# Spreading the operations of a sparse attention stage, and adding squares before they are summed over partitions

## The reference

```python
# first block, layer 0: gated linear attention, 4 heads of 256 values
o = o * lax.rsqrt(jnp.mean(o * o, axis=-1, keepdims=True) + EPS) * g_out
# first block, layer 1: sparse attention, 16 heads of 64, 4 key heads
kv = (hn @ w_kv).reshape(Bsz, S, 6, NSA_KV_HEADS, NSA_HEAD_DIM).transpose(2, 0, 3, 1, 4)
k_cmp = compress_blocks(kv[0], pe_k, wk1, wk2)
v_cmp = compress_blocks(kv[1], pe_v, wv1, wv2)
o = gates[0] * o_cmp + gates[1] * o_sel + gates[2] * o_win
# second block, both layers: 4 heads of difference attention, 8 of stick-breaking
w = probs(qb1, k1) - lam * probs(qb2, k2)
o_diff = (rms_norm(o_diff, subln) * (1.0 - lam_init)).reshape(b, s, DIFF_WIDTH)
a = jnp.where(mask, jnp.exp(log_beta + after), 0.0)
```

## Time and profile before

| | |
|---|---|
| three runs | 2820.82, 2820.78, 2819.22 us; median 2820.78 |
| profiled execution | 2820.03 us, its span 2818.3 us |
| instructions | 39309 |
| PE busy | 2794.5 us, 99% |
| POOL busy | 2043.4 us, 73% |
| VectorE busy | 1328.5 us, 47% |
| ScalarE busy | 816.2 us, 29% |
| mean granted clock of TensorE | 0.998 |

### The profile page before, as it was taken

The page is one execution under the profiler, slowest core; times in us unless marked ns, Lnnn a source line. Parts: engine busy times, 40 slices in busy tenths (PEclk is TensorE's granted clock), DMA queues, the critical chain, the costliest instruction groups (busy, mean ns, idle before and its releaser), DMA issues.

```text
span 2818.3 us, 39309 instructions
## 1 busy us (share of the span) xinstructions
PE 2794.5 (99%) x14380; PEld 2257.1 (80%) x14380; DVE 1328.5 (47%) x1878; ACT 816.2 (29%) x1470; POOL 2043.4 (73%) x2353
## 2 busy tenths in 40 slices
PE   9999999999999999999999999999999999999999
PEld 7888888888766888888877788888887777888887
DVE  4945666044575576604765553231074545533201
ACT  3342222024475222202435422110043444211101
POOL 7958998768655788877855587777785456877774
PEclk9999999999999999999999999999999999999999
DMA  4213223233200333332212223332332222332232
GB/s 153 77 53 105 96 96 94 96 96 120 68 2 2 98 97 97 97 97 94 86 60 68 68 91 96 97 97 97 97 97 68 66 62 82 95 96 95 96 96 96
DMA packets 66507, 242.59 MB, mean 86 GB/s; under 512 B 7504, under 2 KB 7632, under 8 KB 66384
## 3 DMA queue, kind: packets, MB, share of 16 engines
q1 hardware_dynamic: 66384, 240.95, 26.6%
HBM read 238.82 MB, written 2.10 MB: 85 GB/s over the span
## 4 chain that ended last, share of the span: by engine, by line
PE 96%; DVE 2%; ACT 1%; issue 1%; POOL 0%; DMA 0%; SPq 0%; DVEq 0%; ACTq 0%
PE bank L545 28%; PE bank L547 28%; PE bank L546 28%; PE bank L1018 1%; PE bank L942 1%; PE bank L1199 1%; PE bank L1115 1%; PE bank L1158 1%; PE bank L960 1%; PE bank L1171 1%; PE bank L1096 1%; ACT n_P L1551 1%; PE bank L599 0%; DVE ss L1805 0%; PE bank L1086 0%
## 5 line engine op out<-in xcount | busy, mean ns | idle before, releaser
L504 POOL TENSOR_TENSOR w_lo<-w_raw,w_hi 128x256 fp32r<-128x256 f32 x1780 | 1480.9, 863 | 49.6 <-ACT w_hi L1458 14.6
L545 PE MATMUL bank<-XH,w_hi 128*128 128x512 f32 x2416 | 957.0, 396 | 3.6 <-POOL w_lo L504 2.0
L547 PE MATMUL bank<-XH,w_lo 128*128 128x512 f32 x2416 | 942.5, 390 | 0.0
L546 PE MATMUL bank<-XL,w_hi 128*128 128x512 f32 x2416 | 941.8, 390 | 0.0
L501 POOL CAST w_hi<-w_raw 128x1024 fp32r<-128x1024 f32 x437 | 484.0, 1108 | 622.3 <-DMA w_raw<-weights_dram 621.4
L545 PEld LDWEIGHTS bank<-XH,w_hi 128*128 128x128 f32 x2416 | 454.4, 188 | 104.4 <-issue 9.9
L547 PEld LDWEIGHTS bank<-XH,w_lo 128*128 128x128 f32 x2416 | 454.3, 188 | 96.4
L546 PEld LDWEIGHTS bank<-XL,w_hi 128*128 128x128 f32 x2416 | 454.8, 188 | 93.8 <-issue 2.6
L1820 DVE TENSOR_TENSOR X<-X,bank 128x512 f32<-128x512 f32 x63 | 43.1, 684 | 512.5 <-PE bank L547 512.2
L547 PE MATMUL bank<-hid_h,w_lo 128*128 (+1 forms) x704 | 273.9, 389 | 0.0
L545 PE MATMUL bank<-hid_h,w_hi 128*128 (+1 forms) x704 | 273.9, 389 | 0.0
(11 more groups left out here) (368 smaller groups left out, 3303.3 us busy)
## 6 DMA issues: line engine op xcount, KB each, us to landing
w_raw<-weights_dram SPq DMA_DIRECT2D x445, 512.0 KB, 3.4
x_tok<-x_dram SPq DMA_DIRECT2D x4, 512.0 KB, 5.0
out_dram<-y_tok SPq DMA_DIRECT2D x4, 512.0 KB, 4.1
const_sb<-consts_dram SPq DMA_DIRECT2D x1, 834.0 KB, 12.0
par_sb<-params_dram SPq DMA_DIRECT2D x1, 665.0 KB, 10.5
masks_in<-masks_dram SPq DMA_DIRECT2D x1, 640.0 KB, 13.0
w_raw<-weights_dram SPq DMA_DIRECT2D x2, 256.0 KB, 6.4
y_gain<-gain_out_dram SPq DMA_DIRECT2D x1, 512.0 KB, 4.5
```

Of the source, the lines that this page charges most:

```text
L504: ins = nc.gpsimd.tensor_tensor(w_lo[s][:, rows, :], w_raw[s][:, rows, :], w_hi[s][:, rows, :].bitcast(F32), ALU.subtract)
L545: nc.tensor.matmul(out_ap, w_hi[slot][:, j, :], xh, start=start, stop=False)
L546: nc.tensor.matmul(out_ap, w_hi[slot][:, j, :], xl, start=False, stop=False)
L547: return nc.tensor.matmul(out_ap, w_lo[slot][:, j, :], xh, start=False, stop=stop)
```

## The change

It has five parts. The diff follows, cut to its core.

1. GLA: VectorE adds the two squared tiles of each head, and PE sums four tiles in place of eight.
2. kv stage: the tile units come one place earlier against the compression units; ScalarE's high parts are made later among its other work; PE's last compression unit stands between two turns of values.
3. Query stage and row loop: score rows 2 and 3 are issued in the middle of the last query tile, with their maxima and exponentials ahead of that tile's eviction. The steps of rounds 2 and 3, the turns and the late swaps get other rows.
4. Difference attention: ScalarE keeps the squares in f32 and makes a rounded copy, VectorE the rest, and PE sums both with two matmuls in fp32r against minus one (ScalarE's Ln takes the opposite scale). PE waits also for the rest (`osql`). For head 3 the subtraction is put ahead of the stick-breaking loop on VectorE.
5. `stats(MID)` moves from k = 2 to k = 6 of its tile.

```diff
-KV_UNIT = [START["kv"] + (t if t < 5 else 2 * t - 4) for t in range(U_NSA_KV)]
-CMP_UNIT = [START["kv"] + 5 + 2 * n for n in range(U_CMP)]
+KV_UNIT = [START["kv"] + (t if t < 6 else 2 * t - 5) for t in range(U_NSA_KV)]
+CMP_UNIT = [START["kv"] + (6 + 2 * n if n < 7 else 19) for n in range(U_CMP)]
...
-        CMP_TURN_ROW = (24, 64)
+        CMP_TURN_ROW = (22, 58)
+        SWAP_ROW = (27, 28, 33, 34, 51, 52, 57, 58)
...
                 for k in range(KT):
+                    if between and k == KT // 2:
+                        between(2)
...
-                    if k == 2 and norm == MID:
+                    if k == 6 and norm == MID:
                         stats(norm)
...
                         for h in range(H4):
-                            pe.wait_ge(gs["osq"], 2 * h + 2)
-                            for j in range(2):
-                                mm = nc.tensor.matmul(bank[4 + h][:, :], ones_m, g_osq[:, 2 * h + j, :], start=j == 0, stop=j == 1)
-                            mm.then_inc(gs["on"], 1)
+                            pe.wait_ge(gs["osq"], 8 + h + 1)
+                            nc.tensor.matmul(bank[4 + h][:, :], ones_m, g_osq[:, 2 * h, :], start=True, stop=True)\
+                                .then_inc(gs["on"], 1)
...
-                    if t >= 4:
-                        compress(t - 4)
+                    if t >= 5:
+                        compress(t - 5)
                     if t - 1 in (6, 7, 10):
                         v_turn(t - 1)
+                compress(7)
                 v_turn(11)
...
-                    tile(u0 + t, t % 4, XH2, XL2, ns["xl2"] if t == 0 else None)
+                    tile(u0 + t, t % 4, XH2, XL2, ns["xl2"] if t == 0 else None,
+                         between=scores if t == 8 else None)
...
                     pe.wait_ge(hs["osq"], 4 * ly + h + 1)
+                    pe.wait_ge(hs["osql"], 4 * ly + h + 1)
                     if h:
                         pe.wait_ge(hs["ors"], 4 * ly + h)
-                    nc.tensor.matmul(bank[6][:, :], ones_m, h_osq[:, :], start=True, stop=True).then_inc(hs["on"], 1)
+                    nc.tensor.matmul(bank[6][:, :], negones_r[:, :], h_osq_hi[:, h, :], start=True, stop=False)
+                    nc.tensor.matmul(bank[6][:, :], negones_r[:, :], h_osq_lo[:, :], start=False, stop=True).then_inc(hs["on"], 1)
...
                 for t in range(4):
-                    if t == 2:
+                    if t == 3:
                         compression_high(0)
...
+                k_swap(0)
                 compression_high(1)
-                k_swap(0)
-                compression_high(2)
                 k_swap(1)
                 k_doubled(0)
+                compression_high(2)
+                k_doubled(1)
                 compression_high(3)
...
-                for q in range(2, NSA_ROWS + 8):
-                    if q in (15, 51):
-                        cmp_exp(2 + q // 51)
-                    if 34 <= q < 38:
-                        late_swap(6, q - 34)
-                    if 58 <= q < 62:
-                        late_swap(7, q - 58)
+                for q in range(4, NSA_ROWS + 8):
+                    if q in (13, 49):
+                        cmp_exp(2 + q // 49)
+                    if q in SWAP_ROW:
+                        late_swap(6 + SWAP_ROW.index(q) // 4, SWAP_ROW.index(q) % 4)
...
-                    nc.scalar.activation(h_osq[:, :], bank[3][:, :], ACT.Square).then_inc(hs["osq"], 1)
+                    own(nc.scalar.activation(h_osq[:, :], bank[3][:, :], ACT.Square))
+                    nc.scalar.activation(h_osq_hi[:, h, :], h_osq[:, :], ACT.Copy).then_inc(hs["osq"], 1)
...
+                for h in range(H4):
+                    dve.wait_ge(gs["osq"], 8 + h)
+                    V.tensor_tensor(g_osq[:, 2 * h, :], g_osq[:, 2 * h, :], g_osq[:, 2 * h + 1, :], ALU.add).then_inc(gs["osq"], 1)
                 for f in range(5):
                     gated(f)
...
                 for e in range(8):
+                    if e == 7:
+                        score_weights(0)
+                        score_weights(1)
+                        score_max(2)
+                        score_max(3)
                     dve.wait_ge(s_used, START["nsa_q"] + 1 + e + 1)
...
+                def squares_low(h):
+                    dve.wait_ge(hs["osq"], 4 * ly + h + 1)
+                    V.tensor_tensor(h_osq_lo[:, :], h_osq[:, :], h_osq_hi[:, h, :].bitcast(F32), ALU.subtract).then_inc(hs["osql"], 1)
+
...
                     combine(n)
+                    if n >= 5 and (n - 5) % TT == 0:
+                        squares_low((n - 5) // TT)
...
                 k0 = SB_HEADS * ly
+                squares_low(DIFF_HEADS - 1)
                 for h in range(SB_HEADS):
```

More of the change, by code:

```diff
@@ L355, in build @@
         h_osq = at("h_osq", [P, T], F32, o_sq)
+        h_osq_hi = at("h_osq_hi", [P, 4, T], F32R, o_A + 16384)
+        h_osq_lo = at("h_osq_lo", [P, T], F32R, o_sq)
         h_ors = at("h_ors", [P, T], F32, o_sq + T)
@@ L418, in build @@
             "evac", "rot", "rope", "vT", "vc", "gate", "lp", "lsum", "le", "lam", "s", "mx", "exp", "w", "t", "tc", "pv",
-            "sqs", "skd", "osq", "on", "ors", "od", "odh", "odl", "z", "ln", "soft", "sphi", "sp", "cum", "a", "spv", "osc", "osh", "osl", "mevac", "mt", "m", "mh",
+            "sqs", "skd", "osq", "osql", "on", "ors", "od", "odh", "odl", "z", "ln", "soft", "sphi", "sp", "cum", "a", "spv", "osc", "osh", "osl", "mevac", "mt", "m", "mh",
             "ml")}
@@ L575, in first_tiles, with tile @@
                 mm.then_inc(s_used, 1)
-            def tile(u, b, xh, xl, k_sem=None, k_base=0, norm=None):
+            def tile(u, b, xh, xl, k_sem=None, k_base=0, norm=None, between=None):
                 for k in range(KT):
+                    if between and k == KT // 2:
+                        between(2)
                     if u:
@@ L986, in nsa @@
                         cmp_turn(1, 2)
-                        scores(2)
                 for q in range(4, NSA_ROWS + 6, 2):
@@ L1482, in k_doubled @@
                     ins.then_inc(ns["kd"], 1)
+                k_swap(0)
                 compression_high(1)
-                k_swap(0)
-                compression_high(2)
                 k_swap(1)
                 k_doubled(0)
+                compression_high(2)
+                k_doubled(1)
                 compression_high(3)
-                k_doubled(1)
                 v_copy(0)
@@ L1493, in nsa @@
                 v_copy(1)
+                k_swap(2)
                 compression_high(5)
-                k_swap(2)
-                compression_high(6)
                 k_swap(3)
                 k_doubled(2)
+                compression_high(6)
+                k_doubled(3)
                 compression_high(7)
-                k_doubled(3)
                 v_copy(2)
@@ L1560, in nsa @@
                         cmp_exp((e - 3) // 2)
-                score_exp(0)
-                score_exp(1)
+                for q in range(4):
+                    score_exp(q)
                 cmp_copy(1, 2)
@@ L1749, in d_norm @@
                     act.wait_ge(hs["od"], 4 * ly + h)
-                own(nc.scalar.activation(h_ors[:, :], bank[6][:, :], ACT.Ln, bias=eps_col, scale=1.0 / (2 * DH)))
+                own(nc.scalar.activation(h_ors[:, :], bank[6][:, :], ACT.Ln, bias=eps_col, scale=-1.0 / (2 * DH)))
                 nc.scalar.activation(h_ors[:, :], h_ors[:, :], ACT.Exp, scale=-0.5).then_inc(hs["ors"], 1)
@@ L2266, in nsa @@
                         score_max(1)
-                    if e == 7:
-                        score_weights(0)
-                        score_weights(1)
                 def late_cos(e):
@@ L2280, in late_sum @@
                     V.tensor_tensor(n_q[:, e, :], n_rot[e % 2][:, :], n_t1[:, :], ALU.add).then_inc(ns["rope"], 1)
-                for q in range(2, NSA_ROWS + 9):
+                for q in range(3, NSA_ROWS + 9):
                     if q == 7:
                         cmp_scores(3)
+                    if q in (9, 45):
+                        cmp_max(2 + q // 45)
                     if q in (11, 47):
-                        cmp_max(2 + q // 47)
-                    if q in (13, 49):
-                        cmp_less(2 + q // 49)
+                        cmp_less(2 + q // 47)
+                    if q in (15, 51):
+                        cmp_sums(2 + q // 51)
                     if q in (17, 53):
-                        cmp_sums(2 + q // 53)
-                    if q in (21, 57):
-                        cmp_weights(2 + q // 57)
+                        cmp_weights(2 + q // 53)
                     if q in (39, 63):
@@ L2306, in nsa @@
                         V.tensor_copy(transposed_rows(m), turned_bank(m)).then_inc(ns["tcd"], 1)
-                    if q < NSA_ROWS:
+                    if 4 <= q < NSA_ROWS:
                         score_max(q)
-                    if 3 <= q <= NSA_ROWS:
+                    if q <= NSA_ROWS:
```

## The result

Measured over 20 runs of each kernel, the changed one takes 2824.32 us (2822.17 to 2826.69) and the one before 2819.87 (2815.95 to 2824.03): ratio 1.0016 [1.0010, 1.0022]. So it is a little slower, by about 4.5 us or 0.16%, and that is outside the noise of these runs. I had forecast 3.5 faster, 2817.3, with a range of 2814 to 2821. The profiled execution after took 2822.92 us (span 2821.1), 2.9 more than the profiled one before.

The account below looks back on a forecast made before the run. PE was taken to bound the kernel, through what it issues and waits for. Terms -1.6 - 5.0 - 0.8 - 2.6 - 0.7 - 3.0 + 10.2 = -3.5 gave median 2817.3 us (own range 2814 to 2821; 8 in 10: 2810.5 to 2824.5).

Parts of the forecast that it names:

- Head 3, +10.2: Difference attention, two layers: subtraction ahead of VectorE's stick-breaking loop delays sp, PE pauses and the clock falls; +5.1 each.
- rival (a): Head 3's pause is cheap, short chain and clock holds: 2.9 each instead of 5.1, median 2812.9; chance 0.27.
- the long chain: Head 3: VectorE's chain from L2431 to the end of L2439 at its upper end, 6.4 us; bound 7.1 a layer.
- kv stage, -5.0: Unit order of the kv stage: PE's waits for POOL, n_yh and the V copy go; -5.0, between -5.8 and -1.5.
- Rival (c): Early waits only move, POOL or ScalarE late elsewhere; kv and sparse stages bring 2.6, not 8.4; median 2823.1, chance 0.12.
- GLA, displaced queue "at nothing, up to +1": Gatings and norms behind VectorE's GLA adds come some 2.7 us later, covered by VectorE's gaps: nothing, up to +1.
- The term for the sums: GLA square sums: PE runs 4 matmuls instead of 8 but waits for VectorE's first add; -1.6, from -3.2 to +0.3.
- rival (d): VectorE's adds cost GLA what it gains: 1.6 us more; no chance of its own, within the first case's range.
- Row loop, -2.6: Spread swaps fit ScalarE's gaps, -1.0; the fourth round's turn moves to a row with idle time, about -1.9; -2.6.
- Heads 0 to 2, -3.0: Difference attention, two layers: two rounded matmuls (0.45) replace one f32 matmul (0.95) on PE; -0.5 six times, -3.0.
- Query stage -0.35 against -0.8: Score rows 2 and 3 inside the query tile: the 0.9 wait for n_P goes; -0.8, from -1.6 to +0.3.
- MID -0.7 against -0.7: Norm sum of MID four steps later in its tile: its 0.6 wait for ss goes; -0.7, from 0 to -0.8.

Follow-up runs that it names:

- Experiment 2: Kernel before, with VectorE only waiting for the squares of head 3 ahead of its stick-breaking loop, no instruction added: 2825.78 us, ratio 1.0023.
- Experiment 5: Changed kernel, with ScalarE's high part of the second compression unit (unit 1) made ahead of the first swap: 2824.5 us, ratio 1.0018 to the kernel before.
- Experiment 7: Changed kernel, with only ScalarE's high part of the first compression unit (unit 0) made a turn earlier, as it was: 2823.67 us, ratio 1.0015 to the kernel before.
- Experiment 8: Changed kernel, with compression unit 0's high part a turn earlier and unit 1's ahead of the first swap: 2819.02 us, ratio 0.9999 to the kernel before.
- Experiment 6: Changed kernel, with late swaps at rows 39, 40, 63, 64 instead of 33, 34, 57, 58: 2822.84 us, ratio 1.0011 to the kernel before.
- experiment 3: Changed kernel, with head 3's subtraction moved into head 0's step, behind sp and its tile's eviction: 2820.18 us, ratio 1.0003 to the kernel before.
- experiment 4: Changed kernel, with the four GLA adds ahead of VectorE's eviction of tile 21, on their own semaphore: 2820.94 us, ratio 1.0002 to the kernel before.

## Why the prediction was wrong

**Head 3, +10.2: right.** Measured +4.5 and +5.2. The working held part by part: subtraction ahead of sp, a pause of 3.87 (forecast 4.5), chain 4.3 (4.9), and a slower clock behind it in both layers. Experiment 2 shows the mechanism without any of the new instructions. (Two of its bounds don't come out of its terms: a short chain without the clock gives 2.6, where rival (a) counts 2.9, and the long chain 6.6, where I wrote 7.1.) I had this price and set against it 13.7 us of gains, of which 7.0 came, and 2.0 more were lost in GLA. So the error is in the gains.

**kv stage, -5.0: failed, it brought 2.0.** The failed step is "POOL has that tile ready at about 627 and the next at about 641". The first held (625.81). The next I dated by POOL's own work alone and left out what POOL waits for, ScalarE's high parts. The diff makes them later: it puts `compression_high(0)` one turn later and `compression_high(1)` behind the swap, which waits for VectorE. POOL, with nothing to do from 625.8 on, began the compression unit at 633.24, and PE's tile was ready at 650.26. Experiments 5, 7 and 8 show that these two places, together, are the cause; with both the stage brings 2.0 + 3.9 = 5.9, about my own upper end of 5.8. The waits for n_yh and the V copy did go as forecast. Rival (c), with a chance of 0.12, has this outcome almost to the number: it gave the kv stage, query stage and row loop 2.6 in place of 8.4, and they brought 2.8. It said that POOL or ScalarE would be late, and it was ScalarE. What I had named in its favour, that POOL was busy throughout, was not the reason: POOL stood idle.

**GLA, displaced queue "at nothing, up to +1": failed, +2.0.** The term for the sums is right (-1.6, measured -1.7). What failed is the cover that I counted on behind them, "VectorE had gaps of 1.8 us before the last evictions". The gaps took in most of the adds, but the other instructions grew by 2.0, and the last low part came 2.5 later. The slack at the output product was 2.5 and PE came 1.7 earlier. I had not read that slack at all. This is rival (d), which I had put inside the forecast.

**Row loop, -2.6: failed, -0.45.** The failed step is "two and two with six rows between them fit the gaps", -1.0: they cost 0.78 each at the second pair of both late rotations, and the old places gave back only 0.34 and 1.05, so this part came to +0.2. Experiment 6 takes both costs away by moving these pairs alone. The turn was mis-sized too, -0.8 in place of -1.6 (-1.9, and 0.3 for a late copy). The pause of 1.9 went, but the rows behind it cost 0.7 more than they had behind a pause, with a wait of 0.19 for n_P at 858.36 that was not there, and each of the two turns costs 0.2 more in its new row.

**Heads 0 to 2, -3.0: mis-sized, -1.8.** The mechanism was right. From L1110 to L1122 it is 0.56 in place of 0.95, a gain of 0.39 and not 0.5: the second rounded matmul takes 0.32 to the 64-row matmul behind it, where the first takes 0.24. Six of these are 2.3; 0.5 us came back in later steps, 0.3 of it in one step of the second layer, near 2197 us. I have not traced them.

**Query stage -0.35 against -0.8, MID -0.7 against -0.7.** Both within their bounds. In the first the split tile cost 0.2 as forecast, but the turns of the first row behind it take 0.87 in place of 0.61.

Added up: the kv stage 3.0, the row loop 2.15, GLA 1.9, heads 0 to 2 1.2, the query stage 0.45, less 0.5 at head 3 and 0.2 elsewhere, is 8.0. The median after is 7.0 above the forecast, because the kernel before itself measured 0.9 lower over 20 runs than over the three that I started from.

## What to carry to other kernels

When an edit changes the order of units, redo the dates of every engine that feeds the new order, and of what each of them waits for: a helper that stands idle can be late because of its own supplier. Here two of its inputs came late in turn, and only mending both helped. A gain on PE is worth at most the slack at the next thing PE takes from another engine, less what the edit adds to that engine's queue: with 2.5 us of slack in GLA, 3.4 gained and 0.2 added brought 2.0, and 1.7 gained and 2.5 added lost 0.3. To read that slack, count both engines from one instruction that both traces share. And an operation that waits must not stand ahead of a chain that decides: a subtraction of 0.7 us that waited 10.6 cost 4.5, and 5.2 in the other layer.

## What the hardware showed

A pause of PE of 1.9 to 2.9 us was followed by a granted clock near 0.5 or by 1.00 in the same place of the same or an equal instruction stream (the row loop's 1.9: 1.00 before, 0.54 in experiment 2; head 3 in experiment 2: 0.59 in one layer, 1.00 in the other). It is worth about 1.6 us each time, and at the start, where it fell in the profile before and not after, 1.5: enough to make a single profiled execution misleading at this size. After the two of 3.9 us it fell both times in the changed kernel, and in the five others that kept them (experiments 4 to 8). I had counted on the clock holding after 1.9.

A VectorE copy within SBUF was held up by a cast on POOL. In experiment 3 the first copy of 128x128 began at 1486.46, within POOL's cast (1485.92 to 1487.45), and ended at 1487.53, after 1.07 us; the second took 0.21. POOL's cast, which had begun within VectorE's subtraction (1485.86 to 1486.55), took 1.53 there and 1.04 later. The Trainium skill (SBUF — State Buffer, section "SBUF: two separate sides") tells of exclusion for a whole instruction between GpSimd and a VectorE instruction that has two SBUF inputs or runs in a two-port performance mode, which it says an f32 copy from SBUF to SBUF triggers. The trace agrees: the copy ended 0.08 us after the cast, and the cast took 0.5 longer behind the subtraction.
